# Narrower and wider projections, scale factors moved into the turning products, sums of squares on VectorE, and a first group by halves: one change to a two-block float32 kernel

## The reference, cut to what matters

```python
# first block (one layer)
f = swiglu(rmsnorm(h, g1), w_gate, w_up, w_down);   h = h + 0.5 * rmsnorm(f, post1)   # boundary p1 -> x1
m = token_mixer(rmsnorm(h, g2), ...);               h = h + rmsnorm(m, post2)         # boundary p2 -> x2
f = swiglu(rmsnorm(h, g3), ...);                    h = h + 0.5 * rmsnorm(f, post3)   # boundary p3 -> x3
h = h + rmsnorm(sigmoid(rmsnorm(h, g4) @ w_pg) * (p @ w_pp), post4)                   # boundary p4 -> x4
# second block (one layer)
u = rmsnorm(h, norm_mix) @ w_in_2      # split in 17 parts: convolution, sparse attention, dilated attention
h = h + concat(y_conv, y_sparse, y_dilated) @ w_out_2
h = h + sigmoid(h @ w_ple_gate_2) * (p_2 @ w_ple_proj_2)
out = rmsnorm(h, norm_final)
```

## Time and profile before

| what | value |
|---|---|
| median of 3 runs | 1583.26 us (1582.64 to 1583.91) |
| the profiled execution | 1583.49 us, of which span 1581.8 us |
| busy share of PE, DVE, ACT, POOL | 99%, 47%, 37%, 11% |
| share of PE in the chain that ended last | 95% |
| granted PE clock | 0.999 of full |
| DMA | 145.13 MB, 92 GB/s on average |

### The profile page before, as it was taken

How to read it: one execution, slowest core, us unless ns; L and a number is a source line. 1 busy time by engine, 2 the same in 40 slices (tenths; PEclk the granted TensorE clock), 3 DMA queues, 4 the chain that set the end, 5 groups by cost and what they waited for, 6 DMA issues and landing times.

```text
span 1581.8 us, 19212 instructions
## 1 busy us (share of the span) xinstructions
PE 1569.2 (99%) x7900; PEld 1279.3 (81%) x7900; DVE 749.8 (47%) x1110; ACT 590.5 (37%) x952; POOL 166.7 (11%) x167
## 2 busy tenths in 40 slices
PE   9999999999999999999999999999999999999998
PEld 7888888888888877888888888888888877777887
DVE  6444223436545433434844323433746455567645
ACT  5332222236432233324632223322665342434335
POOL 3311001101013400110111100110102000000100
PEclk9999999999999999999999999999999999999999
DMA  4433233323323322333333333333235322121322
GB/s 150 138 92 101 93 93 103 97 93 90 96 82 94 94 80 80 95 103 96 94 94 94 94 106 94 93 97 103 80 94 128 91 46 54 49 54 50 111 80 93
DMA packets 123735, 145.13 MB, mean 92 GB/s; under 512 B 18776, under 2 KB 86496, under 8 KB 123648
## 3 DMA queue, kind: packets, MB, share of 16 engines
q1 hardware_dynamic: 122080, 138.56, 29.1%
q0 software_dynamic: 1568, 5.34, 1.3%
HBM read 141.78 MB, written 2.10 MB: 91 GB/s over the span
## 4 chain that ended last, share of the span: by engine, by line
PE 95%; DVE 2%; ACT 2%; DMA 1%; POOL 0%; issue 0%; SPq 0%; DVEq 0%; ACTq 0%; POOLq 0%
PE G L57 86%; PE X L57 6%; PE X L60 2%; PE G L60 1%; POOL act_t L69 0%; ACT whi L63 0%; ACT sq_t L63 0%; DMA raw<-in_ffn_w_up_dram 0%; ACT xh L63 0%; DVE xl L72 0%; DVE wlo L69 0%; DMA raw<-in_w_in_dram 0%; DVE f L69 0%; DVE h L72 0%; DVE pcmp L69 0%
## 5 line engine op out<-in xcount | busy, mean ns | idle before, releaser
L69 DVE TENSOR_TENSOR wlo<-raw,whi 128x1024 fp32r<-128x1024 f32 (+2 forms) x259 | 312.2, 1214 | 499.7 <-ACT whi L63 499.1
L57 PE MATMUL G<-xh,whi 128*128 128x512 f32 (+1 forms) x1192 | 467.1, 392 | 0.6 <-DVE act_t L69 0.6
L57 PE MATMUL G<-xl,whi 128*128 128x512 f32 (+1 forms) x1192 | 461.4, 387 | 0.7 <-DVE xl L72 0.7
L57 PE MATMUL G<-xh,wlo 128*128 128x512 f32 (+1 forms) x1192 | 460.6, 386 | 0.0
L63 ACT ACTIVATE whi<-raw 128x1024 fp32r<-128x1024 f32 (+2 forms) x259 | 266.3, 1038 | 465.3 <-DMA raw<-in_ffn_w_up_dram 155.6
L57 PEld LDWEIGHTS G<-xl,whi 128*128 128x128 f32 x1192 | 223.8, 188 | 47.0 <-DVE xl L72 1.2
L57 PEld LDWEIGHTS G<-xh,whi 128*128 128x128 f32 x1192 | 224.0, 188 | 44.8 <-issue 1.4
L57 PEld LDWEIGHTS G<-xh,wlo 128*128 128x128 f32 x1192 | 224.1, 188 | 43.4
L69 POOL TENSOR_TENSOR tmp_t<-tmp_t,act_t 128x512 f32<-128x512 f32 x52 | 73.0, 1405 | 588.2 <-DVE tmp_t L69 472.0
L57 PE MATMUL G<-whi,ah 128*128 128x512 f32 x320 | 124.6, 389 | 0.0
L57 PE MATMUL G<-whi,al 128*128 128x512 f32 x320 | 124.5, 389 | 0.0
(11 more groups left out here) (260 smaller groups left out, 1767.9 us busy)
## 6 DMA issues: line engine op xcount, KB each, us to landing
raw<-in_w_in_dram SPq DMA_DIRECT2D x55, 512.0 KB, 3.7
raw<-in_ffn_w_gate_dram SPq DMA_DIRECT2D x88, 256.0 KB, 2.9
raw<-in_ffn_w_up_dram SPq DMA_DIRECT2D x88, 256.0 KB, 3.1
raw<-in_ffn_w_down_dram SPq DMA_DIRECT2D x44, 512.0 KB, 3.7
raw<-in_w_in_dram SPq DMA_DIRECT2D x12, 384.0 KB, 3.3
raw<-in_w_out_a_dram SPq DMA_DIRECT2D x8, 512.0 KB, 3.8
raw<-in_w_out_b_dram SPq DMA_DIRECT2D x8, 512.0 KB, 3.7
raw<-in_w_o_dram SPq DMA_DIRECT2D x8, 512.0 KB, 3.8
```

The source lines that it names most:

```text
L57: return self.e.matmul(out, lhs, rhs, start=start, stop=stop) if self.e else Idle()
L69: return self.e.tensor_tensor(*a) if self.e else Idle()
```

## The change

It has six parts.

1. **Turning products.** `norm_f` is gone from ACT and DVE. `factor_f` now also makes `turner[i]`, the identity times the block's factor (DVE, 128 by 128), and `turn_f` multiplies by `turner` with an ordinary float32 matmul in place of the 128 by 128 transposition with the identity.
2. **Widths.** The 128 sparse values move from `dv` (512 wide to 384) to `vg` (146 wide to 274).
3. **Squares.** At all four boundaries DVE adds up both halves (`sum_pair`, `sum_last` for half 0, one unit's `split_lo`, then half 1). POOL adds no squares any more.
4. **First norm.** ACT squares the rows of `x` with a running sum (`square_rows`, four instructions of 128 by 1024), and takes the root from these sums; POOL's `gather` and PE's `total` for it are gone.
5. **First two units by halves.** The first group runs its first four channel tiles one after the other over all four banks (`by_k`), with each of the first two units split in two halves of 512 columns; tiles 2 to 7 are turned between them. SP waits for the first piece of `x` before it sends the second. `fill(10)` becomes `fill(3)`.
6. **Banks.** `pg2` and `pp2` use the banks in the order 1, 2, 3, 0 (`GB`).

```diff
-        for name, parts, ends in (("dv", [(3346, 3730), (1792, 1920)], 3), ("dq", [(2578, 2962)], 2), ("dk", [(2962, 3346)], 2),
-                                  ("vg", [(2048, 2194)], 3)):
+        for name, parts, ends in (("dv", [(3346, 3730)], 3), ("dq", [(2578, 2962)], 2), ("dk", [(2962, 3346)], 2),
+                                  ("vg", [(1792, 1920), (2048, 2194)], 3)):
...
+                if by_k:
+                    del chunks[0:2]
+                    for u in range(4):
+                        n, kk = first + u // 2, u % 2
+                        hi, lo, key = x[u]
+                        for wi, xv in ((0, hi), (1, hi), (0, lo)):
+                            pe.wait_ge(w_lo if wi else w_hi, n if kk else (n, "half"))
+                            ready(x_lo if xv is lo else x_hi, key, None)
+                            for m in order:
+                                w = parts_of(n)[wi][:, kk * wid + m * 128:kk * wid + (m + 1) * 128]
+                                t = pe.matmul(G[m][:, 0:T], w, xv, u == 0 and wi == 0 and xv is hi, False)
+                        if kk:
+                            t.then_inc(*unit_read.event(n))
+                        else:
+                            hooks[2 * (u // 2), "half"]()
...
-                            pe.wait_ge(normed_dve if b > 1 and st != "p4" else normed_act, (st, i))
-                            t = pe.transpose(X[b][:, (k % 2) * 256 + (i % 2) * 128:(k % 2) * 256 + (i % 2) * 128 + 128],
-                                             ftok[:, i, k * 128:(k + 1) * 128], ident[:, :])
+                            pe.wait_ge(turner_done, (st, i))
+                            t = pe.matmul(X[b][:, (k % 2) * 256 + (i % 2) * 128:(k % 2) * 256 + (i % 2) * 128 + 128],
+                                          ftok[:, i, k * 128:(k + 1) * 128], turner[:, i, :], True, True)
...
-            fill(10)
-            turn(2)
-            turn(3)
...
+            fill(3)
             hooks = pre_hooks("s0")
-            hooks[0, 1] = lambda: (turn(4), turn(5))
-            hooks[2, 1] = rest
+            hooks[0, "half"] = lambda: (turn(2), turn(3))
+            hooks[2, "half"] = lambda: (turn(4), turn(5))
+            hooks[4, 0] = lambda: (turn(6), turn(7))
...
+            g_free[:] = g_free[1:] + g_free[:1]
...
-            def norm_f(st, i):
-
-                act.wait_ge(r_done, (st, i))
-                of = ftok[:, i, :] if st == "p4" else ft(i, 0)
-                act.activation(of, of, ACT.Copy, scale=rpost[:, i:i + 1]).then_inc(*normed_act.event((st, i)))
...
+            def square_rows(i):
+                for n in range(4):
+                    act.wait_ge(x_in[n], "x")
+                if i:
+                    act.wait_ge(squared, ("s0", i - 1))
+                act.activation(sq_t[:, :, :].rearrange("p a t -> p (a t)"), xrow[:, i, :], ACT.Square,
+                               accum_out=ss0[:, i:i + 1]).then_inc(*squared.event(("s0", i)))
...
                 dve.reciprocal(rpost[:, i:i + 1], rpost[:, i:i + 1]).then_inc(*r_done.event((st, i)))
-
-            def norm_f(st, i):
-
-                if st == "p4":
-                    return
                 dve.wait_ge(r_done, (st, i))
-                dve.tensor_scalar(ft(i, 1), ft(i, 1), rpost[:, i:i + 1], None, ALU.mult).then_inc(*normed_dve.event((st, i)))
+                dve.tensor_scalar(turner[:, i, :], ident[:, :], rpost[:, i:i + 1], None, ALU.mult).then_inc(*turner_done.event((st, i)))
...
-                sum_pair(1, 0, 1)
-                sum_pair(1, 2, 3)
-                sum_last(1)
-                ahead(first + 2)
+                for half in (0, 1):
+                    sum_pair(half, 0, 1)
+                    sum_pair(half, 2, 3)
+                    sum_last(half)
+                    if half == 0:
+                        ahead(first + 2)
...
-            ffn("ffn1", (1,), {(2, 1): first_squares})
-            gather_first("s1", "x1")
+            ffn("ffn1", (1,), None)
...
+                if n == 0:
+                    sp.wait_ge(x_in[0], "x")
```

More of the change, by code:

```diff
@@ L169, in two_blocks @@
         post, _ = sb("post", [128, 16], F32)
+        turner, _ = sb("turner", [128, 4, 128], F32)
         poolw = at("poolw", [128, 4, 2, 256], F32, m_o)
@@ L511, in gemm @@
                                     if by_token:
-                                        t = pe.matmul(G[m][:, 0:wid], xv[:, m * 128:(m + 1) * 128], wv[wi], start, stop)
+                                        t = pe.matmul(banks[m][:, 0:wid], xv[:, m * 128:(m + 1) * 128], wv[wi], start, stop)
                                     else:
@@ L573, in sums, with factor @@
                     pe.wait_ge(const, "ones")
+                    pe.wait_ge(h_summed, (st, 0))
+                    pe.wait_ge(h_summed, (st, 1))
+                    total(st, "acc", lambda i: acc[:, i // 2, 0, (i % 2) * 128:(i % 2) * 128 + 128], True, True)
+                def factor():
                     if st == "s0":
[L575 to L582, removed]
+                        pe.wait_ge(h_done, ("x0", 7))
                     spread(st)
-                at = (6, 0) if st == "s0" else (6, 1)
-                return {at: sums, (6, 2): factor} if st != "s3" else {at: sums}
+                if st == "s0":
+                    return {(6, 2): factor}
+                return {(6, 1): sums, (6, 2): factor} if st != "s3" else {(6, 1): sums}
             def prepare():
@@ L1208, in ffn, with split_half @@
                 cross(post, pre, gain, head, factor)
+            def split_half(n, kk):
+                act.wait_ge(raw_in[n], n)
+                act.activation(whi[:, n, kk * 512:(kk + 1) * 512], raw[:, n, kk * 512:(kk + 1) * 512],
+                               ACT.Copy).then_inc(*w_hi.event(n if kk else (n, "half")))
+            split_half(0, 0)
             start_hi(0)
-            split_hi()
+            split_half(0, 1)
             start_hi(1)
+            split_half(1, 0)
             start_hi(2)
             start_hi(3)
[L1216 to L1220, removed]
+            split_half(1, 1)
+            split["n"] = 2
+            def square_rows(i):
[5 more added lines that the diff above has]
+                               accum_out=ss0[:, i:i + 1]).then_inc(*squared.event(("s0", i)))
             def second():
+                square_rows(0)
                 start_hi(4)
@@ L1225, in second @@
                 split_hi()
-                first_tiles(4)
             def third():
+                for i in range(1, 4):
+                    square_rows(i)
                 start_hi(6)
@@ L1231, in third @@
                 split_hi()
-                first_tiles(6)
                 split["reach"] = AHEAD
-            hooks = pre_hooks("s0")
-            hooks[0, 0] = second
-            hooks[2, 1] = third
+                act.wait_ge(const, "eps")
+                act.wait_ge(squared, ("s0", 3))
+                act.activation(rtok[:, :], ss0, ACT.Sqrt, bias=eps[:, 0:1], scale=1.0 / D).then_inc(*rooted.event("s0"))
+            hooks = {(2, 0): second, (4, 0): third}
             ffn("ffn1", "p1", "s1", "mix_pre_g", ("v", 0), hooks)
@@ L1365, in scalar @@
                 act.wait_ge(r_done, "s4")
[L1366 to L1368 removed]
+                act.activation(dv[:, i, :], G[i][:, 0:384], ACT.Copy, scale=rtok[:, i:i + 1]).then_inc(*taken.event(("dv", i)))
                 if i == 1:
@@ L1535, in gate_2 @@
                     act.wait_ge(mixed, ("pg2", 0, i))
-                act.activation(acts[i], G[i][:, :], ACT.Sigmoid).then_inc(*activated.event(("pg2", c, i)))
+                act.activation(acts[i], GB[i][:, :], ACT.Sigmoid).then_inc(*activated.event(("pg2", c, i)))
             def square_out(c, i):
@@ L1811, in vector, with split_half @@
             dve.wait_ge(scaled, "g")
+            def split_half(n, kk):
+                dve.wait_ge(w_hi, n if kk else (n, "half"))
+                c = slice(kk * 512, (kk + 1) * 512)
+                dve.tensor_tensor(wlo[:, n, c], raw[:, n, c], whi[:, n, c].bitcast(F32),
+                                  ALU.subtract).then_inc(*w_lo.event(n if kk else (n, "half")))
             turn(0)
             turn(1)
+            split_half(0, 0)
             start_lo(0)
-            split_lo()
             start_lo(1)
+            split_half(0, 1)
             turn(2)
             turn(3)
+            split_half(1, 0)
             start_lo(2)
             start_lo(3)
-            split_lo()
+            split_half(1, 1)
+            split["n"] = 2
             def second():
@@ L1836, in third @@
                 split["reach"] = AHEAD
+                inverse("s0")
             hooks = pre_hooks("s0")
-            hooks[0, 0] = second
-            hooks[2, 1] = third
+            del hooks[6, 0]
+            hooks[2, 0] = second
+            hooks[4, 0] = third
             background.append(prepare())
```

75 lines of the change are left out of this document (14 added, 61 removed).

## The result

| what | before | after |
|---|---|---|
| median of 6 runs each, side by side | 1582.95 us | 1592.11 us (1590.77 to 1595.48) |
| ratio, 95% interval | | 1.0058 (1.0048 to 1.0069) |
| profiled execution, span | 1583.49, 1581.8 us | 1592.36, 1590.6 us |

The kernel became slower by 9.2 us, and the span of its profile by 8.8. The forecast was 1588.7, +5.4, with 1584.5 to 1592.5 as range. The side was right. The time is 0.4 us inside the far edge of the range, and above the 1586.7 to 1590.7 that the likeliest case was given.

A forecast was written before the change was run, and what follows sets the result against it. PE, busy 99% of the span, was taken as the bound; 13.0 + 1.5 - 5.2 - 1.0 - 1.0 + 1.7 - 2.7 - 0.9 = +5.4 us gave 1588.7 us, range 1584.5 to 1592.5.

The forecast's parts named there:

- the likeliest case: The forecast's own sum over the whole kernel, +5.4 us, with its own range 1586.7 to 1590.7 us; chance 0.50.
- The turning products: At four boundaries, 128 float32 products replace 128 transpositions on PE's path: +13.0 us (12.7 to 13.3).
- 0.202 each: Price step for the boundaries' turning products, taken from four 128-wide `spread` products: 0.202 us each, against 0.104 per transposition.
- A: Rival at the 128 turning products: each costs what a transposition costs; sum -7.6 us, 1575.7 us; chance 0.05.
- B: Rival at the turning products: each costs four transpositions, 0.415 us; +27 on the sum, about 1616 us; chance 0.02.
- The lost waits: PE's waits for `xl` at p2, and for ACT's `norm_f` and `xl` at p4, go: -1.0 us at each.
- DVE's queue at p4: At p4 DVE's sums of squares end after PE reaches `total`, so PE waits: +1.7 us (0 to 4).
- -0.65: Forecast in us for the stretch from `total` to `vg`, where the trace showed +1.02.
- The widths: 96 `dv` matmuls narrowed to 384 columns save 5.2 us; 96 `vg` matmuls widened to 274 cost 1.5 us.
- The start: First unit lands at 6.2, first product at 7.6 in place of 11.19: net -2.7 us (0 to -4).
- Banks: At `pg2`, the first tile starts in `G[1]` without the 0.83 us wait for `G[0]`: -0.9 us.
- rival D: The start gives nothing, as the unit lands no earlier or the slow pace lasts: +2.7 us, 1591.4 us; chance 0.13.

## Why the prediction was right, and where its sum was short

**The turning products** set the sign, as forecast. The step "0.202 each" was mis-sized: the row of `spread` is 0.202, the slice of `f` costs 3.48 / 16 = 0.217 and 1.70 / 8 = 0.213 with the change to and from it. Over 128 products that is 4 x (6.88 - 3.25) = 14.5 us, not 13.0; and 128 times the difference of the forecast's own two rows, 0.098, would have been 12.6. A and B are out: the factor over a transposition is 2.1, where the Trainium skill (TensorE: Matmul & The Clock Gate, Terms) speaks of four. The measurement decides.

**The lost waits** were half right. p4's wait for ACT's `f` went; at p2 one of 0.57 became one of 0.23 and did not go, 0.2 us.

**DVE's queue at p4** was right: 1.95 us for the 1.7 forecast, with `xl` at 0.4 a piece without POOL. At p1 the sums end 0.7 us before PE asks, for 1.0 forecast.

**What follows a wait** was missing, and it is the largest miss. The forecast costed the wait at its own length. It costs 1.7 us more through the clock, the difference between -0.65 and +1.02 in the table; in the profile with the wait filled this is gone. None of the rivals had it, and no term of the sum.

**The widths** cost and save per column what was forecast, `dv` 0.174 and `vg` 0.1275 apart. But the -5.2 is no gain by itself: the wide `dv` was the cover of DVE's sums. The forecast had this as a term of its own (+1.7); with the clock the whole is -5.2 + 1.5 + 1.95 + 1.7 = -0.05, nothing.

**The start** agreed to 0.01 us in this pair of profiles. Its steps were right too: the unit landed in time for ACT at 6.25 (forecast 6.2), and the first product and the wait at the third unit came as forecast. But the size is luck of the pair: it was computed from, and compared with, the one execution in which the old start was slow. Against other executions it is 1.2 to 1.7.

**Banks**: 0.83 and its restart, -1.10 for -0.9.

Of the 3.3 us between the two columns of the table, the price of the product is 1.5, the clock 1.7, and the rest (p2 and `vg` +0.2 each, banks -0.2, p1 and p3 -0.1) nearly cancels.

That the time fell inside the range is luck in part. The range reached 1 us beyond rival D's 1591.4, the rival in which the start gives nothing; the start gave what was forecast, and the room was taken by a price 1.5 us too low and by a slow stretch that the forecast did not have.

What stays open: in which executions the clock falls in the attention part. It does in five of the fourteen profiles (three near 1330, two near 1341 to 1348), does not in the profile before or after, and costs 1.6 us each time. Medians of kernels that differ by a microsecond are mixtures of the two. Open too is why 1.95 us at p4 was followed by a low clock and 1.81 and 1.82 us, at a split some 2.5 us ahead of the sums, were not: with one profile each, the length of the wait and the moment at which it falls cannot be told apart. It was not tried to fill or reorder those small products.

## What to carry to other kernels

Price a product of a new kind from the row that is nearest in both operands, and add what entering and leaving it costs. A wait of the bounding engine costs its length and possibly a slow stretch behind it, so shortening the work ahead of a late producer can return nothing; look at the granted clock in half-microsecond windows after every new wait. And read the start of several profiles before crediting a gain there: one late transfer was as large as the gain.

## What the runs showed of the hardware

- The granted clock fell to 0.50 after waits of 1.95, 3.24 and 4.20 us, 0.7 to 1.8 us after PE had begun again and for about 3.4 us each time, and not after waits of 0.89, 1.17, 1.46, 1.81 and 1.82 us, in one profile each. With the 1.95 us filled by ten products it stayed at 1.00.
- It also fell with PE busy, behind small products (48 records, 64x31), in five of fourteen profiles. The Trainium skill (TensorE: Matmul & The Clock Gate, Part 1) calls the throttled state the default that activity lifts, and the number of slow matmuls at a kernel's start variable from run to run. The first agrees with the filled wait here; a variation from run to run these traces show in the middle of the kernel.
- A float32 product of 128 columns costs 0.213 to 0.217 us from start to start where a transposition of the same shape costs 0.104, both at the full clock; with a broadcast column as the stationary operand it costs 0.202.
- With 2 MB of POOL's loads under way (share 1.0, some 200 GB/s) weights landed late in both places tried: ACT stood 6.5 us in one and 13.5 in the other, where in the same profiles it stood for no other unit of `w_in_2` more than 5.0 us.
